# Loading the later experts' weight matrices as two half transfers each

## The reference

```python
g_idx = jnp.argmax(g_logits, axis=-1)              # one group for a token
top_p, top_i = lax.top_k(e_probs, TOP_K)           # two experts in it
for g in range(N_GROUPS):
    h = jax.nn.silu(jnp.einsum('nd,edf->nef', xt, w_gate[g])) * jnp.einsum('nd,edf->nef', xt, w_up[g])
    out = out + jnp.einsum('nef,efd->nd', h * combine[:, g, :, None], w_down[g])
```

## Time and profile before

| what | value |
|---|---|
| profiled execution | 1503.97 us |
| its span, first to last instruction | 1502.2 us (1.8 us of the time lie around it) |
| median of three runs | 1504.05 us |
| PE busy | 1254.7 us, 84% |
| DVE busy | 759.1 us, 51% |
| ACT busy | 478.0 us, 32% |
| transfers | 544.11 MB, 362 GB/s over the span |
| the experts' stage | from about 128 us to 582 us of the span |

### The profile page before, as it was taken

The page is one execution under the profiler, slowest core; times in us unless marked ns, Lnnn a source line. Parts: engine busy times, 40 slices in busy tenths (PEclk is TensorE's granted clock), DMA queues, the critical chain, the costliest instruction groups (busy, mean ns, idle before and its releaser), DMA issues.

```text
span 1502.2 us, 21239 instructions
## 1 busy us (share of the span) xinstructions
PE 1254.7 (84%) x8497; PEld 742.2 (49%) x8497; DVE 759.1 (51%) x1801; ACT 478.0 (32%) x1255; POOL 276.6 (18%) x294
## 2 busy tenths in 40 slices
PE   7999999999799999999999986888666655556566
PEld 7787656565465557987767643345311111111112
DVE  5644222212112215557852876677576665767444
ACT  5843110111001105356653344333323232323223
POOL 0000000000000000100000343344433333333331
PEclk9999999999899999999999998999867687686867
DMA  9548999999999999543461899999999999999996
GB/s 392 207 162 347 428 423 427 423 426 423 425 423 427 424 426 391 217 185 118 164 266 57 314 423 420 422 407 421 421 421 422 421 421 421 421 421 421 422 420 270
DMA packets 65016, 544.11 MB, mean 362 GB/s; under 512 B 6672, under 2 KB 7184, under 8 KB 13200
## 3 DMA queue, kind: packets, MB, share of 16 engines
q1 hardware_dynamic: 26592, 273.85, 44.4%
q0 software_dynamic: 38016, 268.45, 43.2%
q10 hardware_dynamic: 304, 0.39, 0.1%
HBM read 541.62 MB, written 1.05 MB: 361 GB/s over the span
## 4 chain that ended last, share of the span: by engine, by line
PE 51%; DMA 31%; issue 6%; DVE 5%; ACT 4%; POOL 2%; POOLq 0%; DVEq 0%; ACTq 0%; SPq 0%
PE PS L205 49%; DMA AR<-in_uv,CO 24%; DMA AR<-in_w_up 4%; PE PS L215 2%; DVE AR L2516 1%; DMA EX<-in_uv,CO 1%; DMA EX<-in_w_up 1%; POOL AR L2767 1%; DVE LO L201 1%; ACT HI L194 1%; ACT Wk L2411 0%; POOL AR L2739 0%; ACT SM L2405 0%; DVE Wk L1784 0%; POOL AR L2764 0%
## 5 line engine op out<-in xcount | busy, mean ns | idle before, releaser
L205 PE MATMUL PS<-AR,Wk 64*64 64x512 f32 (+3 forms) x2040 | 372.4, 737 | 161.8 <-ACT Wk L2411 150.7
L2516 DVE CUSTOM_DVE_ANT_0 AR<-AR,PS 128x1024 f32<-128x1024 f32 x193 | 234.8, 1219 | 163.9 <-DMA AR<-in_uv,CO 159.6
L205 PEld LDWEIGHTS PS<-AR,Wk 64*64 64x64 f32 (+3 forms) x2040 | 100.6, 160 | 388.2 <-ACT Wk L2411 249.4
L2767 POOL DMA_INDIRECT AR<-in_uv,CO x186 | 178.4, 959 | 279.5 <-PE PS L205 241.5
L205 PE MATMUL PS<-AR 128*64 128x256 f32 (+3 forms) x1656 | 195.1, 387 | 8.8 <-issue 8.0
L205 PEld LDWEIGHTS PS<-AR 128*64 128x64 f32 (+3 forms) x1656 | 122.0, 140 | 86.9 <-issue 34.0
L2401 ACT ACTIVATE RW<-SM 128x2 f32<-128x2 f32 (+1 forms) x132 | 26.9, 204 | 404.7 <-DVE SM L2516 387.6
L319 POOL TENSOR_TENSOR ST<-ST 128x2 f32<-128x2 f32 (+3 forms) x14 | 12.8, 916 | 770.4 <-DVE ST L1183 480.5
L201 DVE TENSOR_TENSOR LO<-AR,HI 128x1024 fp32r<-128x1024 f32 x84 | 99.5, 1225 | 41.6 <-ACT HI L194 41.6
L1059 DVE TENSOR_TENSOR AR<-AR,PS 128x256 f32<-128x256 f32 x32 | 13.5, 421 | 191.8 <-ACT AR L910 191.8
L205 PE MATMUL PS<-Wk,AR 128*128 128x128 f32 (+2 forms) x816 | 96.0, 309 | 0.1
(11 more groups left out here) (350 smaller groups left out, 1873.8 us busy)
## 6 DMA issues: line engine op xcount, KB each, us to landing
AR<-in_w_up SPq DMA_DIRECT2D x24, 2048.0 KB, 14.7
AR<-in_w_down SPq DMA_DIRECT2D x24, 2048.0 KB, 14.7
AR<-in_w_gate SPq DMA_DIRECT2D x24, 2048.0 KB, 14.7
AR<-in_w_in SPq DMA_DIRECT2D x13, 2048.0 KB, 10.1
EX<-in_w_gate SPq DMA_DIRECT2D x4, 2048.0 KB, 15.2
Wk<-in_w_up SPq DMA_DIRECT2D x4, 2048.0 KB, 14.7
EX<-in_w_down SPq DMA_DIRECT2D x4, 2048.0 KB, 14.7
Wk<-in_w_gate SPq DMA_DIRECT2D x4, 2048.0 KB, 14.7
```

Of the source, the lines that this page charges most:

```text
L205: return pe.matmul(o, l, r, start=start, stop=stop, skip_group_check=True)
L2516: t = dve.tensor_tensor_reduce(r, r, P(6 if g < 128 else 2, 2), 1.0, 0.0, ALU.mult, ALU.add, DT[:, g:g + 1])
L2767: pool.indirect_dma_start(RING[k], None, uv, bass.IndirectOffsetOnAxis(ap=IDX[:, g:g + 1], axis=0)).then_inc(g_in[k], 16)
```

## The change

The 88 later pieces are loaded as two transfers of 1 MB. `piece_in_halves` gives such a piece a second semaphore (`ring_second`). `load_halves` waits once for both halves of piece i-3, and then for each half waits until PE is through with that half of piece i-8, and issues it. PE counts a step more in the middle of each product (`gate.h`, `up.h`, `y.h`) and waits there for the second half's semaphore. A half of gate or up is 128 rows of 8 KB, half of each run; a half of down is one of its two runs in each partition. The transfers of b0 and b1 still wait for `arrived`, which now is the first half of eg31 and of ed31.

```diff
+        ring_second = [sem(f"ring_second{i}") for i in range(10)]
+        second, second_uses_of = {}, [0] * 10
...
+        def piece_in_halves(name, src, slot):
+            piece(name, src, slot)
+            second_uses_of[slot] += 1
+            second[name] = (ring_second[slot], 16 * second_uses_of[slot])
...
-            piece(f"eg{ex}", rows8(w_gate[ex]), EXPERT_SLOTS[3 * ex % 8])
+            (piece_in_halves if ex > 2 else piece)(f"eg{ex}", rows8(w_gate[ex]), EXPERT_SLOTS[3 * ex % 8])
...
+        def all_arrived(e, name):
+            e.wait_ge(*arrived(name))
+            if name in second:
+                e.wait_ge(*second[name])
+
+        def load_halves(sp, name, released):
+
+            all_arrived(sp, load_order[load_order.index(name) - 3])
+            src, dst = loads[name][0], raw(name)
+            for k in range(2):
+                cs = slice(2048 * k, 2048 * k + 2048)
+                sp.wait_ge(*released[k])
+                sp.dma_start(dst[:, cs], src[:, cs] if len(src.shape) == 2 else src[:, k, :]).then_inc(
+                    (second[name] if k else arrived(name))[0], 16)
...
-                        sp.wait_ge(*m_pe.at(f"{('gate', 'up', 'y')[j % 3]}{j // 3}"))
-                        load_piece(sp, name, 3)
+                        before = f"{('gate', 'up', 'y')[j % 3]}{j // 3}"
+                        load_halves(sp, name, (m_pe.at(before + ".h"), m_pe.at(before)))
...
+                        if c == 4 and name in second:
+                            pe.wait_ge(*second[name])
                         for j in range(2):
                             t = mm(pe, G[64 * j:64 * j + 64, z:z + 256], xg[:, c, :], w[:, c, 256 * j:256 * j + 256], c == 0, c == 7)
+                        if c == 3:
+                            t.then_inc(*m_pe.up(step + ".h"))
...
+                    if c == 2 and f"ed{ex}" in second:
+                        pe.wait_ge(*second[f"ed{ex}"])
...
+                    if c == 1:
+                        t.then_inc(*m_pe.up(f"y{ex}.h"))
```

More of the change, by code:

```diff
@@ L160, in program @@
         for ex in range(32):
-            piece(f"eg{ex}", rows8(w_gate[ex]), EXPERT_SLOTS[3 * ex % 8])
-            piece(f"eu{ex}", rows8(w_up[ex]), EXPERT_SLOTS[(3 * ex + 1) % 8])
-            piece(f"ed{ex}", w_down[ex].rearrange("(h p c) n -> p h (c n)", h=2, c=2), EXPERT_SLOTS[(3 * ex + 2) % 8])
+            (piece_in_halves if ex > 2 else piece)(f"eg{ex}", rows8(w_gate[ex]), EXPERT_SLOTS[3 * ex % 8])
+            (piece_in_halves if ex > 2 else piece)(f"eu{ex}", rows8(w_up[ex]), EXPERT_SLOTS[(3 * ex + 1) % 8])
+            (piece_in_halves if ex > 1 else piece)(f"ed{ex}", w_down[ex].rearrange("(h p c) n -> p h (c n)", h=2, c=2), EXPERT_SLOTS[(3 * ex + 2) % 8])
         for name, src, slot, half in (
@@ L640, in program @@
             g, k4 = ex // 4, ex % 4
-            m_pe_names += [f"gate{ex}", f"up{ex}", *([f"add{ex - 1}"] if ex else []), *([f"gsum{ex}"] if ex < 31 else []),
-                           f"turned{ex}", *([f"gather{g + 1}.{k4}"] if g < 7 else []), *(["gsum31"] if ex == 31 else []), f"y{ex}"]
+            m_pe_names += [f"gate{ex}.h", f"gate{ex}", f"up{ex}.h", f"up{ex}", *([f"add{ex - 1}"] if ex else []), *([f"gsum{ex}"] if ex < 31 else []),
+                           f"turned{ex}", *([f"gather{g + 1}.{k4}"] if g < 7 else []), *(["gsum31"] if ex == 31 else []), f"y{ex}.h", f"y{ex}"]
             m_act_names += [f"silu{ex}", f"hp{ex}", f"ysh{ex}"]
```

## The result

The changed kernel takes 1506.8 us (median of 17 runs) against 1504.48 us (17 runs): ratio 1.0017, 95% interval 1.001 to 1.0024. That is 2.3 to 2.6 us slower, where 1.25 were forecast, and within the 3.0 us counted as no change. Measured again beside other kernels, it came out at 1.0025, interval 1.0016 to 1.0034, which is 3.8 us and no longer within the 3.0. So it is a small loss, and a real one. The profiled execution has a span of 1505.6 us, 3.4 more than before.

A forecast was written before the change was run, and what follows sets the result against it. Transfers bound the experts' stage, PE close behind. Rows +3.2 us and early start -1.8 us made the stream 1.4 us later, the end 1.25 us later: 1503.97 + 1.25 = 1505.2 us, range 1502.6 to 1509.0.

The forecast's parts named there:

- What bounds the stage: Experts' stage: transfers slower than PE, ending close together; b0's third quarter lets a stream over 0.15 us later delay the end.
- PE by halves: End of experts' stage: up31 ends 0.4 us earlier, at most 0.86 us for PE, not reaching the end.
- gaps in the middle of products: Sign on PE that would show the forecast wrong; no idle time was expected at up30.
- Rows of 8 KB: Gate and up pieces of experts 3 to 31: 0.055 us for each of 58, stream 3.2 us later.
- The early start: First refill, ed2: first half issued when gate0 is half done, stream 1.8 us earlier.
- The sum: Whole kernel: stream +1.4 us at b0, end 1.25 us later, 1505.2 us.
- The forecast's own condition: Stream later by 0.5 to 3.1 us, giving 1504.3 to 1507.0 us; chance 0.55.
- Waits, counts and issues: Added waits and counts on PE and doubled issues on SP in the experts' stage: 0 us each.
- Behind the stage: Work after the experts' sum: the 1.25 us passes on one for one to PE's next big piece.
- Rival 1: Stream: shorter rows cost what b0's quarters cost, or more; stream 5.2 us later, 1509.0 us; chance 0.18.
- Rival 3: Stream: each added transfer pays its start, 0.75 us, 66 us for 88, 1571 us; chance 0.02.
- Rivals 2, 4 and 5: 2: split free, 1503.1 us, 0.17; 4: PE waits cost, up to 1537 us, 0.03; 5: stream quicker, about 1500.9 us, 0.05.

The follow-up runs named there:

- the reorder: Changed kernel with b0's second and third quarter rounded behind `ysh31`, their low parts on DVE behind `ys31`; ratios 1.002 and 1.0019 against the kernel before.
- split only: Changed kernel with the two 1 MB transfers kept, but each piece released and used whole; ratio 1.0035 against the kernel before.
- Start only: Kernel before with halves only for ed2, eg3, eu3 and ed3, later pieces whole; ratios 0.9991 and 0.9998 against the kernel before.
- the reorder alone: Kernel before, pieces whole, with b0's second and third quarter rounded behind `ysh31`; ratio 1.0005 against the kernel before.

## Why the prediction was right, by its steps

*What bounds the stage: right.* Stream and PE end together, and the stream reaches the last `add` through b0's third quarter ahead of `ysh31`. The changed kernel's rows show it (581.20 right behind the rounding), and the reorder takes 1.3 to 1.9 us away. That is the changed kernel's path; with whole pieces eu31's landing holds PE at the same time (split only).

*PE by halves: there, but not as an earlier up31.* Forecast was an up31 that ends 0.4 us earlier than before. Counted from the first matmul it ended 1.7 us later (445.9 against 444.2), since the stream was 3.5 us later and not 1.4; against split only it was 2.5 us earlier. Second halves came late: idle times of 0.54, 0.54 and 0.79 us in the middle of up29, up30 and up31, where none was expected at up30. The prediction had named gaps in the middle of products as a sign of being wrong, and this sign came. As forecast, none of it counted, because b0 came later still.

*Rows of 8 KB: right in kind, too small.* Forecast: 0.055 us for 58 pieces, 3.2 us. Measured: 0.08 for gate, 0.07 for up and 0.02 for down, 29 x 0.08 + 29 x 0.07 + 30 x 0.02 = 5.0 us. The kernel with these rows and one transfer (0.07, 0.06 and 0.01: 4.1 us) puts nearly all of it on the rows. Sums of medians are rough: in the two kernels without an early start, split only and this one, b0's first quarter landed 4.2 us later than before. The step used the difference between down and gate as it stood (0.055), and the rows cost 0.07 to 0.08; down itself changed by 0.01 to 0.02.

*The early start: right in sign, mis-sized.* Forecast 1.8 us, measured 0.5 to 1.1. The first half of ed2 was issued 2.03 us behind the first matmul, ed2 before at 3.71: 1.7 us, nearly as forecast. What the stream made of it stands in the windows of the first and second ten microseconds, before and then changed:

```profile
128.85:138.85 10.00, 9.61 (x82) 7.58 (x84) 3.56 (x12) 2.52 (x5) 0.00 (x0) 1.00 0.51 193
138.85:148.85 10.00, 10.00 (x80) 5.46 (x76) 1.40 (x3) 0.69 (x1) 0.00 (x0) 1.00 1.00 401
```

```profile
127.51:137.51 10.00, 9.60 (x82) 7.58 (x84) 3.55 (x12) 2.54 (x5) 0.00 (x0) 1.00 0.69 255
137.51:147.51 10.00, 10.00 (x80) 5.46 (x76) 1.41 (x3) 0.69 (x1) 0.00 (x0) 1.00 0.97 387
```

The first ten win 62 GB/s, or 1.5 us of the stream; the next ten, in which eu3 is asked for, give 0.3 us back. Start only has the same sum by another way: 218 and 426 GB/s, 1.2 us in all. So the size is shown, and what takes the rest of the 1.7 us is not. The forecast's sentence that SP waits for landings and not for PE from then on misread the trace. In the kernel before, the issues keep PE's pace for longer; those of up pieces come 13.65 us apart, as the experts do, and the first that comes later than PE's pace is at 190.97:

```profile
142.22 0.33 SPq L187 DMA_DIRECT2D AR<-in_w_up  x1
...
155.87 0.33 SPq L187 DMA_DIRECT2D AR<-in_w_up  x1
```

*The sum.* 5.0 - 0.5 to 1.1 gives a stream later by 3.9 to 4.5 us (with the 4.2 of the landings, 3.1 to 3.7); b0's first quarter lands 3.5 us later behind the first matmul (577.72 - 127.51 against 575.58 - 128.85), and 3.9 in the second profile. Less 0.15 this is 3.3 to 3.8, and the stretch is 3.2 and 3.7 longer. With the forecast's +1.4 for the stream it was 1.25. So the two sizes, both wrong the same way, make the difference. The forecast's own condition, a stream later by 0.5 to 3.1 us, was not met; the range held the time because its upper end was taken from b0's quarters. That the end stayed within 3.0 us in the first measurement was partly luck: in the second it did not.

*Waits, counts and issues: nothing, right.* Gate and up, each now with a wait in its middle, still take 7.08 us in the changed kernel, as in the earlier trace rows:

```profile
359.04 7.08 PE L227 MATMUL PS<-AR 128*64 128x256 f32 x64
```

SP's two issues take 0.80 us at a time when two pieces are on the way, and the share stays at 1.01.

*Behind the stage: roughly one for one.* From the last `add` to PE's last long piece ahead of the gathers it is 252.7 us before (580.84 to 833.56) and 253.0 after. But split only, which like the kernel before had no dip of the clock at 660 to 700 us, took 251.4 and so got 1.3 us back. In it ACT's issue of `in_ck` was over at 590.98, 1.6 us later than in the kernel before (589.42), though the last `add` was 3.1 us later. What held that issue in the kernel before was not tried.

*The rivals.* Rival 1 decided from 0.085 us a piece; 0.07 to 0.08 were measured, and the timed loss of 2.3 to 3.8 us stands on both sides of the 3.0 us. Its condition for the price was not met, but the stream was 3.5 and 3.9 us later, beyond the 3.15 at which it decides, because the early start brought less. It was the nearest. Rival 3 is out, and the figure of the Trainium skill beside it (DMA: Bandwidth & Descriptors, section Bandwidth; 341 GB/s for 1 MB) does not hold for this stream: 1 MB transfers run at 420 GB/s when others are queued behind them. Rivals 2, 4 and 5 left no trace.

## What to carry to other kernels

Where a stream of transfers is the limit, cut it only where the stream runs dry, and look at what the cut does to the contiguous runs: here runs of half the length cost 1.2 to 1.6% of the stream, and the distances of the changed kernel and of split only are the same, so early release gained nothing where the issuer waits for landings anyway. Ask of a stream that gets later not only who waits for its own pieces, but what queues behind them and which engine's program order ties that to the critical work; a later rounding of the *next* stage's weights held the last sum of this one. Opening one of two nearly equal paths moves the limit to the other: the reorder alone won nothing, and behind the halves it took 1.3 to 1.9 us off the stretch. And compare stretches between two fixed events, not spans, when the difference is a few microseconds.

## What was not expected of the hardware

Transfers of 1 MB to 64 of the 128 partitions, with the same rows and the same bytes, move at about half the rate: 219 GB/s between 200 and 300 us at a share of 1.01 (232 from 300 to 700), 9.4 to 9.5 us for the two of a piece where two transfers over all 128 partitions take 4.98. Both halves of the partitions were requested, one transfer right behind the other, and still together moved only half as much. Whether the two took turns or ran side by side, each at a quarter, the views do not tell.

The price of a row in a full stream is visible up to 16 KB: 4.90 us for 2 MB in rows of 16 KB, 4.97 in 8 KB, 5.10 in 4 KB.
